# Converting the V blocks of a gated-DeltaNet convolution to token-major rows

## The reference, cut to what matters

```python
qkv, z, b_pre, a_pre = _split(h @ w_in, L1_SPLITS)
qkv = jax.nn.silu(_causal_depthwise_conv(qkv, conv_w))
q, k, v = _split(qkv, [GDN_QK_W, GDN_QK_W, GDN_V_W])
```

## Time and profile before

| | us |
|---|---|
| median of three runs | 2725.53 (2725.23 to 2725.72) |
| span of the profiled execution | 2723.3 |
| PE busy | 2707.9 (99%) |
| DVE busy | 1807.0 (66%) |
| ACT busy | 1412.0 (52%) |
| POOL busy | 94.2 (3%) |

### The profile page before, as it was taken

How to read it: one execution, slowest core, us unless ns; L and a number is a source line. 1 busy time by engine, 2 the same in 40 slices (tenths; PEclk the granted TensorE clock), 3 DMA queues, 4 the chain that set the end, 5 groups by cost and what they waited for, 6 DMA issues and landing times.

```text
span 2723.3 us, 37074 instructions
## 1 busy us (share of the span) xinstructions
PE 2707.9 (99%) x13198; PEld 2252.4 (83%) x13198; DVE 1807.0 (66%) x2538; ACT 1412.0 (52%) x2005; POOL 94.2 (3%) x80
## 2 busy tenths in 40 slices
PE   9999999999999999999999999999999999999998
PEld 7888888888888888888888888888888888888887
DVE  5554678666666666668797978656767666666444
ACT  5444555444444444458787778554454444444443
POOL 0000000000000000001111111000000000000000
PEclk9999999999999999999999999999999999999999
DMA  8564466766666666666464656555666666666664
GB/s 260 155 195 146 154 198 188 200 193 193 192 193 192 193 190 196 194 188 195 151 191 155 186 178 188 170 182 189 193 193 194 192 193 193 193 193 194 209 194 158
DMA packets 264737, 510.93 MB, mean 188 GB/s; under 512 B 20497, under 2 KB 21265, under 8 KB 264353
## 3 DMA queue, kind: packets, MB, share of 16 engines
q1 hardware_dynamic: 260064, 493.91, 60.0%
q0 software_dynamic: 3152, 11.57, 1.3%
q10 hardware_dynamic: 1392, 3.77, 0.4%
HBM read 503.91 MB, written 5.28 MB: 187 GB/s over the span
## 4 chain that ended last, share of the span: by engine, by line
PE 96%; DVE 2%; ACT 0%; issue 0%; DVEq 0%; DMA 0%; SPq 0%; ACTq 0%
PE acc L602 30%; PE acc L603 30%; PE acc L608 30%; PE aux L843 1%; DVE wlo L1541 1%; PE aux L687 1%; PE aux L855 1%; PE aux L848 1%; PE aux L837 0%; PE aux L829 0%; DVE const L1986 0%; DVE arena L1986 0%; DVE arena L2027 0%; DVE arena L2024 0%; DMA x<-in_x 0%
## 5 line engine op out<-in xcount | busy, mean ns | idle before, releaser
L1541 DVE TENSOR_TENSOR wlo<-wraw,whi 128x1024 fp32r<-128x1024 f32 x928 | 1137.0, 1233 | 711.0 <-ACT whi L1052 704.8
L1052 ACT ACTIVATE whi<-wraw 128x1024 fp32r<-128x1024 f32 x928 | 978.5, 1059 | 1101.8 <-PE acc L608 1059.5
L602 PE MATMUL acc<-whi,hT_hi 128*128 128x512 f32 x2624 | 1033.9, 394 | 0.5 <-ACT arena L1062 0.5
L603 PE MATMUL acc<-whi,hT_lo 128*128 128x512 f32 x2624 | 1022.8, 390 | 0.0
L608 PE MATMUL acc<-wlo,hT_hi 128*128 128x512 f32 x2624 | 702.8, 390 | 0.5 <-DVE wlo L1541 0.5
L608 PEld LDWEIGHTS acc<-wlo,hT_hi 128*128 128x128 f32 x2624 | 492.0, 188 | 103.7 <-DVE wlo L1541 1.3
L602 PEld LDWEIGHTS acc<-whi,hT_hi 128*128 128x128 f32 x2624 | 493.3, 188 | 101.9 <-ACT arena L1062 0.8
L603 PEld LDWEIGHTS acc<-whi,hT_lo 128*128 128x128 f32 x2624 | 493.4, 188 | 100.1
L602 PE MATMUL acc<-whi,arena 128*128 128x512 f32 x1072 | 417.2, 389 | 0.0
L603 PE MATMUL acc<-whi,arena 128*128 128x512 f32 x1072 | 417.0, 389 | 0.0
L608 PE MATMUL acc<-wlo,arena 128*128 128x512 f32 x1072 | 286.5, 389 | 0.0
(11 more groups left out here) (269 smaller groups left out, 1202.3 us busy)
## 6 DMA issues: line engine op xcount, KB each, us to landing
wraw<-in_l_w_in SPq DMA_DIRECT2D x304, 512.0 KB, 4.3
wraw<-in_l_w_gate SPq DMA_DIRECT2D x176, 512.0 KB, 4.3
wraw<-in_l_w_up SPq DMA_DIRECT2D x176, 512.0 KB, 4.3
wraw<-in_l_w_down SPq DMA_DIRECT2D x176, 512.0 KB, 4.3
wraw<-in_l_w_out SPq DMA_DIRECT2D x96, 512.0 KB, 4.5
arena<-decay_sums POOLq DMA_DIRECT2D x16, 512.0 KB, 5.1
o_rounds<-arena POOLq DMA_DIRECT2D x3, 1024.0 KB, 5.5
arena<-o_rounds ACTq DMA_DIRECT2D x3, 1024.0 KB, 5.2
```

The lines of the kernel that those rows point to most:

```text
L602: nc.tensor.matmul(pair[m], hi[:, k, tok], wh, start=first, stop=False)
L603: nc.tensor.matmul(pair[m], lo[:, k, tok], wh, start=False, stop=False)
L1052: nc.scalar.activation(whi[:, s, :], wraw[:, s, :], ACT.Copy).then_inc(hi_done, 1)
L1541: V.tensor_tensor(wlo[:, s, :], wraw[:, s, :], whi[:, s, :].bitcast(F32), ALU.subtract).then_inc(lo_done, 1)
```

## The change

V0 and V1 no longer go through PE and back. K and Q are as before. For a V block:

- GpSimd issues DMAs (`lags`) that copy the block's rows of `qkv` into three tiles, shifted one, two and three partitions later, since partitions are tokens. Each lag takes two DMAs: 127, 126 or 125 partitions of 2 x 512 elements, and the 1, 2 or 3 rows that cross from the first 128 tokens to the second. Another DMA (`taps`) broadcasts four rows of 512 weights to all partitions. Tiles for two of the lags and for the weights lie in `x`, which holds the residual; so `store_x` writes `x` (2 MB) to DRAM at the start of the phase and `load_x` reads it back after the last round. The third lag lies in `const`.
- DVE (`v_conv`) does four multiplies and three adds of 128x1024 and a memset of 3x512, in four parts: for V0 in slots 2, 3, 4 and 5; for V1 in slots 21, 23, 24 and 27.
- ACT applies SiLU (`v_rows_silu`, slots 7 and 28) and then writes the rows times beta (slots 13 and 30) from SBUF. Its `tap` of V is gone.
- PE's four runs of 8 transposes per round are gone, with the waits that went with them. Slot 32 waits for `v_rows`.

```diff
+            def store_x():
+                pool.wait_ge(xs_copied, 8)
+                pool.dma_start(x_dram[:, :], xflat).then_inc(x_stored, 16)
+                pool.wait_ge(x_stored, 16)
+                nc.gpsimd.memset(row_lag[0][0:1, 0, :], 0.0)
+                nc.gpsimd.memset(row_lag[1][0:2, 0, :], 0.0).then_inc(lag_zero, 1)
...
+            def taps(r, b):
+                n, col = V_BLOCK(r, b), P * conv_tile(r, b)
+                if n:
+                    pool.wait_ge(v_sum, n)
+                pool.dma_start(tap_rows, A["conv_rows"][:, col:col + NB].rearrange("(a w) n -> a w n", a=1).to_broadcast([P, CW, NB])
+                               ).then_inc(taps_in, 16)
+            def lags(r, b):
+                n = V_BLOCK(r, b)
+                pool.wait_ge(acc_read[b % 2], (BLOCK0["l1"] + 4 * r + b) // 2 + 1)
+                if n:
+                    pool.wait_ge(v_rows, n)
+                for lag in range(1, CW):
+                    dst = row_lag[lag - 1]
+                    pool.dma_start(dst[lag:, :, :], qkv[0:P - lag, :, v_cols(b)]).then_inc(v_lags, 16)
+                    pool.dma_start(dst[0:lag, 1, :], qkv[P - lag:, 0, v_cols(b)]).then_inc(v_lags, 16)
...
             keep_x("dn0")
+            store_x()
+            taps(0, V0)
             pool.wait_ge(gate_step, GATE_AT["sums_exp"])
...
             decay_rows(0)
+            lags(0, V0)
             decay_columns(0)
...
-                if s == 0:
-                    if r:
-                        pe.wait_ge(end_dve, END_DVE(r - 1, "o1"))
-                    conv_transposes(V0, aux[1])
...
-                    pe.wait_ge(conv_sum, TOK_AT(r, V0))
                     products(4, aux[1])
-                if s == 10:
                     pe.wait_ge(tok_copy, TOK_AT(r, K))
-                    token_major(V0, aux[0])
-                if s == 15:
-                    pe.wait_ge(tok_copy, TOK_AT(r, V0))
                     conv_transposes(Q, aux[0])
...
-                if s == 27:
-                    pe.wait_ge(kq_mask, r + 1)
-                    conv_transposes(V1, aux[0])
...
-                if s == 31:
-                    pe.wait_ge(conv_sum, TOK_AT(r, V1))
-                    token_major(V1, aux[0])
...
+                def v_rows_silu(b):
+                    act.wait_ge(v_sum, V_BLOCK(r, b) + 1)
+                    nc.scalar.activation(flat(row_lag[2]), flat(row_lag[2]), ACT.Silu).then_inc(v_silu, 1)
...
                 if s == 28:
-                    tap(V1)
+                    v_rows_silu(V1)
...
-                if s == 31:
-                    silu(V1)
-                if s == 32:
+                if s == 30:
                     act.wait_ge(et_set, r + 1)
                     value_rows(V1)
...
+                def v_conv(b, part):
+                    n, v = V_BLOCK(r, b), qkv[:, :, v_cols(b)]
+                    tap = lambda lag: tap_rows[:, CW - 1 - lag, :].unsqueeze(1).to_broadcast([P, M, NB])
+                    if part == 0:
+                        dve.wait_ge(taps_in, 16 * (n + 1))
+                        dve.wait_ge(v_lags, 16 * V_LAGS * (n + 1))
...
+                        V.tensor_tensor(v, v, tap(0), ALU.mult)
+                        V.tensor_tensor(row_lag[0], row_lag[0], tap(1), ALU.mult).then_inc(v_step, 1)
+                    if part == 1:
+                        V.tensor_tensor(row_lag[1], row_lag[1], tap(2), ALU.mult)
+                        V.tensor_tensor(row_lag[2], row_lag[2], tap(3), ALU.mult).then_inc(v_step, 1)
+                    if part == 2:
+                        dve.wait_ge(v_step, V_STEPS * n + 1)
+                        V.tensor_tensor(v, v, row_lag[0], ALU.add).then_inc(v_step, 1)
+                        dve.wait_ge(v_step, V_STEPS * n + 2)
+                        V.memset(row_lag[2][0:CW - 1, 0, :], 0.0)
+                        dve.wait_ge(v_step, V_STEPS * n + 3)
+                        V.tensor_tensor(v, v, row_lag[1], ALU.add).then_inc(v_step, 1)
+                    if part == 3:
+                        dve.wait_ge(v_step, V_STEPS * n + 4)
+                        V.tensor_tensor(row_lag[2], v, row_lag[2], ALU.add).then_inc(v_sum, 1)
...
-                if s == 2:
-                    conv(V0)
+                if 2 <= s < 6:
+                    v_conv(V0, s - 2)
...
+                if s == 21:
+                    v_conv(V1, 0)
                 if s == 22:
                     conv(Q)
+                if s in (23, 24):
+                    v_conv(V1, s - 22)
...
                 if s == 27:
-                    conv(V1)
+                    v_conv(V1, 3)
```

More of the change, by code:

```diff
@@ L162 @@
 D_AT = counts(0, 1)
-TOK_AT = counts(K, V0, Q, V1)
-CONV_TR_AT = lambda r, b: b + 1 if r == 0 else 3 * r + 1 + b
+TOK_AT = counts(K, Q)
+CONV_TR_AT = lambda r, b: 1 if b == K else r + 2
+V_BLOCK = lambda r, b: 2 * r + (b == V1)
+V_STEPS, V_LAGS = 4, 2 * (CW - 1)
 GRAM_AT = counts("kk", "kq")
@@ L256, in build @@
         qkT = at(28 * KB, [P, 8, SEQ])
-        vT = C["decay"].rearrange("p (t n) -> p t n", n=SEQ)
+        row_lag = [xflat[:, 2 * NB * l:2 * NB * (l + 1)].rearrange("p (m n) -> p m n", m=M) for l in range(2)]
+        row_lag.append(C["decay"].rearrange("p (m n) -> p m n", m=M))
+        tap_rows = xflat[:, 4 * NB:8 * NB].rearrange("p (w n) -> p w n", w=CW)
         k_turned = at(36 * KB, [P, 4, SEQ])
@@ L298, in build @@
         aux = [ctx.enter_context(nc.psum_tensor(f"aux{i}", [P, 2 * NB], F32)) for i in range(2)]
-        conv_in = lambda r, b: flat(k_turned) if b == K and r else (aux[0], aux[1], aux[0], aux[0])[b]
+        conv_in = lambda r, b: flat(k_turned) if b == K and r else aux[0]
         aux4 = [aux[i // 2][:, (i % 2) * NB:(i % 2 + 1) * NB] for i in range(4)]
@@ L346, in build @@
         conv_silu = sem("conv_silu")
+        x_stored = sem("x_stored")
+        x_back = sem("x_back")
+        lag_zero = sem("lag_zero")
+        taps_in = sem("taps_in")
+        v_lags = sem("v_lags")
+        v_step = sem("v_step")
+        v_sum = sem("v_sum")
+        v_silu = sem("v_silu")
+        v_rows = sem("v_rows")
         tok_tr = sem("tok_tr")
@@ L556, in gdn @@
                 nc.gpsimd.memset(T[:], 0.0)
+                taps(r, V1)
+                lags(r, V1)
                 if r == ROUNDS - 1:
@@ L574, in gdn @@
                     pool.wait_ge(lev_psum, LEVEL_PSUM(r, "TT64_1"))
+                    taps(r + 1, V0)
                     decay_rows(r + 1)
+                    lags(r + 1, V0)
                     decay_columns(r + 1)
@@ L1349, in value_rows @@
                             n = HV * c + 4 * (b == V1) + h
-                            a = nc.scalar.activation(v_tok[int(b == V1)][:, c, h, :], aux[0][:, c * NB + h * P:c * NB + (h + 1) * P], ACT.Copy,
-                                                     scale=small(3, n, 1))
-                    a.then_inc(tok_copy, 1)
+                            a = nc.scalar.activation(v_tok[int(b == V1)][:, c, h, :], row_lag[2][:, c, head(h)], ACT.Copy, scale=small(3, n, 1))
+                    a.then_inc(v_rows, 1)
                 def level_copy(step, dst, rows, cols):
@@ L1380, in gdn @@
                 if s == 7:
-                    silu(V0)
+                    v_rows_silu(V0)
+                    if r == ROUNDS - 1:
+                        load_o(0)
                 if s == 9:
@@ L1459, in qkv_out @@
                     act.wait_ge(k_turns, r - 1)
+                elif r and q in (V0, V1):
+                    act.wait_ge(v_sum, V_BLOCK(r - 1, q) + 1)
                 elif r:
@@ L1583, in add @@
                     dve.wait_ge(xhi_done, n + 4 * norm)
+                    if norm == 3 and isinstance(n, int) and n == 0:
+                        dve.wait_ge(x_back, 16)
                     V.tensor_tensor(xs[:], acc[parity][:, :, :], x[:, :, bass.ds(n * NB, NB)], ALU.add
```

24 lines of the change are left out of this document (17 added, 7 removed).

## The result

| | us |
|---|---|
| before, median | 2725.53 |
| changed, median of 5 runs | 2933.51 (2931.35 to 2936.89) |
| ratio | 1.0763, 95% interval 1.0751 to 1.0775 |
| predicted | 2743.5 (2730 to 2765) |

The account below looks back on a forecast made before the run. PE and, in slots 0 to 25 of each round, DVE with 0.9 us to spare bound the kernel. Rounds of 4.0, 4.4, 4.4, 4.2 plus 1.0 at the start add 18.0 us to the 2723.3 span: median 2743.5, range 2730 to 2765.

Parts of the forecast that it names:

- the landing of the lag copies: First round: V0's copies land at 1239, making DVE 3.3 us late; later copies are issued at least 20 us ahead.
- the one-engine copy: Rival, chance 0.12: the 127-partition copy runs on one DMA engine, up to 45 us or 30; total about 2800.
- The start: Phase's first units: writing x and the first weight rows cost 1 us, bounds 0 and 3.
- The load of `x`: Reading x back falls where leads are long and costs nothing.
- ACT's wait in slot 29: Slot 29: PE waits another 1.1 us a round for the q64 copy queued behind ACT's SiLU of V1.
- PE's saving: Four transpose runs in each of four rounds go, 0.92 us each: 14.7 us.
- The new DVE instructions: V convolution on DVE: seven 128x1024 operations at 1.13 us each and a memset of 0.5, 8.4 us for V0.
- PE's waits for `wlo`: Sign of being right: PE waits for wlo in slots 20 to 24, some 7 to 8 us a round.
- The lateness of 5.1 at slot 25: Before slot 25 DVE is 6.0 us late against 0.9 of lead, so PE is 5.1 late.
- A whole round: Net cost of the four rounds in order: 4.0, 4.4, 4.4 and 4.2 us.
- The weights starve: Rival, chance 0.10: copies hold back PE's 512 KB weight units, 3 us a round; total 2755.
- The saving shows: Rival, chance 0.06: DVE keeps up, all 14.7 us of PE's saving stay; total 2710.8.

Follow-up runs that it names:

- The bystanders: e3_bystander and e4_bystander_split: the kernel before plus store and load of x and lag copies that nobody reads; 2837.96 and 2732.53 us.
- e5_taps_late: e1_split with the first broadcast of weight rows issued behind round 0's decay rows, not right behind the store of x; 2784.99 us, ratio 1.0221.
- e6_silu_late: e1_split with ACT's SiLU of V1 moved from slot 28 to slot 30, behind the q64 copies; 2769.93 us, ratio 1.0160.
- e1_split: The changed kernel with each large lag copy cut into 112 partitions and the 15, 14 or 13 left; 2782.09 us, ratio 1.0206.
- e7_v1_behind: e6_silu_late with all of DVE's parts for V1 in slots 27 and 28, none in 21, 23 and 24; 2777.11 us.
- e4_bystander_split: The kernel before plus store and load of x and lag copies cut at 112 partitions, read by nobody; 2732.53 us, ratio 1.0025.
- e11_ceiling_b: The changed kernel without lag copies, weight rows, store and load of x, with one DVE add per V block instead of eight instructions; 2713.35 us, ratio 0.9955.
- e3_bystander: The kernel before plus x written out and read back and the changed kernel's uncut lag copies, read by nobody; 2837.96 us, ratio 1.0412.
- e8_rearranged: The changed kernel's arithmetic with lag copies cut at 112 partitions and DVE's, ACT's and GpSimd's work and transfers reordered; 2755.24 us, ratio 1.0106.

## Why the prediction was wrong

**The step that failed** is the landing of the lag copies in "For 1.5 MB this gives 1238.8 to 1244.7; I take 1239" and "Later lag copies are issued at least 20 us ahead of their use": the forecast priced the copies by the decay loads, which have 128 partitions, and put the one-engine copy among the rivals at 0.12. In the changed kernel the first block's landed at 1277, and the seven later blocks held DVE for 111.6 us. The rival gave the copy's price right in kind (30 to 45 us; 28.4 measured with the issue) and too low for the whole kernel (2800): it left out that V0's blocks of the later rounds wait as well, and that the clock falls. The three shapes stood in the diff and no transfer like them in the trace, so the forecast's price had no row of its shape behind it, and the rival deserved more than 0.12. The shape is worth 151 us of the 208.

**The clock had no term.** The sum counted waits of PE and nothing after them. In the changed kernel PE's work takes 48.9 us longer, some 42 of them by the clock. With split copies it is 22.6 us (2716.0 less 2693.4); 31.1 us of PE's work are at 0.50 there, which makes an estimated 15.5 of the 22.6. That is nearly as much as the forecast was short in idle time (49.4 against 32.7, below).

**The start and the load of `x`.** The start: 1.0, bounds 0 to 3; measured 8.5 from unit 0 to 9. The bystanders (1.7 and 3.9 with the store alone) and `e5_taps_late` put it on both transfers, the broadcast more than the store. The load of `x`: nothing; in four of the variants it crowds with the loads of `o_rounds`, and 7.1 to 9.3 us are lost at one unit.

**ACT's wait in slot 29**: 1.1 a round forecast, 12.2 in four rounds with split copies. The order of events was as told. Its size was off in part since V1's last add took 1.7 us longer beside GpSimd's product, in three of the four rounds; in the last it took 1.14 us, and PE still waited 2.5. A wait of 2.8 costs the clock too. `e6_silu_late` shows that the order is the cause, not that all of it can be had back.

**What was right.** PE's saving: 14.7, measured 14.5. The new DVE instructions: most are 1.13 to 1.14 apart (longer beside GpSimd's work), with 0.41 from the memset to the next row. PE's waits for `wlo` with split copies are 28.6 us, 7.1 a round, as said (7 to 8), though partly in slots 8 to 10 and not all in 20 to 24. The lateness of 5.1 at slot 25: in the third round of `e1_split`, counted from slot 0, it is 5.7, and 2.6 in `e7_v1_behind`. In the others it is 7.6 to 8.7, with waits for weights or copies in it. A whole round still costs 13.3, 11.8, 9.6 and 15.9 us by the table, where 4.0, 4.4, 4.4 and 4.2 were forecast: in the third, 5.1 of the 9.6 come in slot 29, where 1.1 was said. The forecast's idle time, 18.0 + 14.7 = 32.7, stands against 49.4 measured with split copies.

**The rivals.** "The weights starve" at 3 us a round was wrong for copies in that place (`e4_bystander_split`: nothing in three rounds). With the weight rows beside them it shows: PE waits 2.0 us for `whi` in slot 20 of the second round of `e1_split`, and the same mechanism took back V1's gain in `e7_v1_behind`. "The saving shows" needs work that costs nothing (`e11_ceiling_b`).

**Open**: how the 112 us of `e3_bystander` split into held-up weights and ACT's wait for the copies, what PE's busy time holds beyond the clock, and whether `e8_rearranged` would gain all of its 7.1 us with only the load of `x` moved: no run moves it alone.

## What to carry to other kernels

Before a transfer between partitions is priced by its bytes, look at its number of partitions: of the six tried here 127 is by far the worst, and 112 + 15, one after the other, move the same rows in 6.5 us instead of 28.4. A wait of PE can be paid twice, once as idle time and once at the lower clock. New work belongs where its engine waits for PE anyway, with its transfers issued a good part of a round ahead and not beside other large ones; a saving on PE alone is worth only what the other engines let through.

## What the hardware showed unexpectedly

- A GpSimd copy of 127 partitions x 1024 fp32 elements: 28.4 us, 3.6 of them the issue; of 128, 3.5 and 0.87. Ten weight units in another queue: 39.3 us beside it, 23.1 alone.
- 4 MB of other loads issued within 3 us: a weight unit of 512 KB lands 12.7 us after its issue; the median in the changed kernel is 4.4.
- PE after a wait of 2.85 us: granted clock 0.50 for 6.8 us, from within the wait on, and PE's next run 3.67 us where it had been 2.08.
- DVE's add of two SBUF tiles took 2.84 us beside a GpSimd product that itself took 2.99 instead of 1.90; alone 1.13. The Trainium skill (SBUF — State Buffer, "SBUF: two separate sides") says that of a DVE operation with two SBUF inputs and a GpSimd operation that reads SBUF, the one that starts first holds the shared port pair and the other fully blocks. The row of 2.84 agrees: the product ended at 1475.97, and the row behind the add comes 1.0 later. So do V0's third and fourth multiply, which take 2.03 us each beside GpSimd's masking in all four rounds of the changed kernel, and 1.14 in `e1_split`, where the masking comes at another time.
